# Down-projection weights of experts 0 to 14 loaded as full rows, their four column blocks combined together

## The reference, cut to what matters

```python
xe = jax.vmap(lambda hb, ib: hb[ib])(h, idx)                       # 16 experts x 32 tokens x 2048
hid = jax.nn.silu(jnp.einsum('becd,edf->becf', xe, w_gate)) * jnp.einsum('becd,edf->becf', xe, w_up)
ye = jnp.einsum('becf,efd->becd', hid, w_down) * gates[..., None]  # w_down: 16 x 1024 x 2048
# combine: zeros((n, d)).at[idx].add(ye); then h = h + mod[5] * that, and a last RMS norm
```

## Time and profile before

| | us |
|---|---|
| median of three runs | 1775.41 |
| lowest, highest | 1771.18, 1778.32 |
| span of the profiled execution (first to last instruction) | 1773.1 |
| PE busy | 1491.6 |
| DVE busy | 711.5 |
| ACT busy | 341.8 |
| POOL busy | 99.1 |

### The profile page before, as it was taken

How to read it: one execution, slowest core, us unless ns; L and a number is a source line. 1 busy time by engine, 2 the same in 40 slices (tenths; PEclk the granted TensorE clock), 3 DMA queues, 4 the chain that set the end, 5 groups by cost and what they waited for, 6 DMA issues and landing times.

```text
span 1773.1 us, 20259 instructions
## 1 busy us (share of the span) xinstructions
PE 1491.6 (84%) x7818; PEld 829.8 (47%) x7818; DVE 711.5 (40%) x1134; ACT 341.8 (19%) x591; POOL 99.1 (6%) x83
## 2 busy tenths in 40 slices
PE   2998999999999999998777788777887787877776
PEld 0557778877888777864122133211341232322112
DVE  1437677676767876653122032112211220321013
ACT  2433234233333345551000000000000000000001
POOL 0000000002340422000000000000000000000001
PEclk8999999999999999997887797778788877987787
DMA  9999656755746674578999999999999999999996
GB/s 340 381 363 267 240 193 240 277 195 201 250 166 235 208 269 149 191 308 312 420 416 416 417 419 416 415 418 419 415 416 419 418 416 415 419 417 416 417 420 253
DMA packets 155267, 593.24 MB, mean 335 GB/s; under 512 B 17838, under 2 KB 18214, under 8 KB 121390
## 3 DMA queue, kind: packets, MB, share of 16 engines
q1 hardware_dynamic: 144576, 580.95, 84.1%
q10 hardware_dynamic: 10606, 11.05, 2.1%
HBM read 589.80 MB, written 2.16 MB: 334 GB/s over the span
## 4 chain that ended last, share of the span: by engine, by line
PE 52%; DMA 33%; DVE 4%; SPq 4%; issue 2%; ACTq 2%; ACT 2%; POOL 0%; DVEq 0%; POOLq 0%
DMA ring_c<-in_w_up 10%; DMA ring<-in_w_up 10%; DMA ring_b<-in_w_down 8%; PE bank L530 7%; PE bank L532 7%; PE bank L531 7%; PE bank L849 5%; PE bank L784 4%; SPq L430 4%; PE bank L814 4%; DMA ring<-in_w_gate 2%; PE bank L526 2%; PE bank L835 2%; PE bank L528 2%; PE bank L527 2%; PE bank L775 2%
## 5 line engine op out<-in xcount | busy, mean ns | idle before, releaser
L814 PE MATMUL bank<-ring,xg 128*32 128x512 f32 x1536 | 243.7, 732 | 115.1 <-DMA ring<-in_w_gate 52.8
L1235 DVE TENSOR_TENSOR whl<-ring,whl 128x512 fp32r<-128x512 f32 x280 | 214.2, 769 | 150.8 <-ACT whl L916 150.0
L916 ACT ACTIVATE whl<-ring 128x512 fp32r<-128x512 f32 x280 | 176.3, 630 | 304.6 <-PE bank L532 237.2
L530 PE MATMUL bank<-whl,uh 128*128 128x512 f32 x512 | 209.8, 410 | 5.4 <-DVE vv L1262 1.7
L532 PE MATMUL bank<-whl,ul 128*128 128x512 f32 x512 | 200.3, 391 | 0.0
L531 PE MATMUL bank<-whl,uh 128*128 128x512 f32 x512 | 200.2, 391 | 0.0
L1531 DVE COPY gup<-bank 128x512 f32<-128x512 f32 x32 | 22.1, 691 | 440.8 <-PE bank L814 440.8
L814 PEld LDWEIGHTS bank<-ring,xg 128*32 128x32 f32 x1536 | 36.7, 117 | 289.3 <-DMA ring<-in_w_up 138.2
L1218 DVE SCALAR_TENSOR_TENSOR part<-ring,csT,part 128x1024 f32<-128x1024 f32 x120 | 160.4, 1336 | 0.1
L1125 ACT ACTIVATE gup<-bank 128x512 f32<-128x512 f32 x32 | 18.7, 597 | 635.4 <-PE bank L814 635.4
L784 PE MATMUL bank<-yy,gcur 128*128 128x512 f32 x256 | 122.6, 611 | 14.2 <-DVE yy L1542 14.2
(11 more groups left out here) (223 smaller groups left out, 1514.8 us busy)
## 6 DMA issues: line engine op xcount, KB each, us to landing
ring<-in_w_gate SPq DMA_DIRECT2D x128, 1024.0 KB, 20.6
ring<-in_w_mod SPq DMA_DIRECT2D x96, 1024.0 KB, 7.2
ring<-in_w_up SPq DMA_DIRECT2D x64, 1024.0 KB, 23.9
ring<-in_w_down SPq DMA_DIRECT2D x64, 1024.0 KB, 24.0
ring<-in_w_in SPq DMA_DIRECT2D x54, 1024.0 KB, 5.3
ring_b<-in_w_up SPq DMA_DIRECT2D x32, 1024.0 KB, 26.7
ring_c<-in_w_up SPq DMA_DIRECT2D x32, 1024.0 KB, 26.0
ring_b<-in_w_down SPq DMA_DIRECT2D x32, 1024.0 KB, 19.1
```

The source lines that it names most:

```text
L530: mm(ps, hi[:, k, cols], wh, start=k == 0, stop=False)
L814: last = mm(bank[2 * m + half][32 * quad:32 * quad + 32, :], xg[:, 2 * j + kk, CAP * ei:CAP * ei + CAP], w[:, kk, 512 * half:512 * half + ...
L916: a(whl[:, cidx % (AHEAD + 1), 0, :], slot_buf(slot[n])[:, 512 * (k % 4):512 * (k % 4) + 512], ACT.Copy).then_inc(hi_split, 1)
L1235: v.tensor_tensor(whl[:, cidx % (AHEAD + 1), 1, :], slot_buf(slot[n])[:, 512 * (k % 4):512 * (k % 4) + 512], whl[:, cidx % (AHEAD + 1), 0, ...
```

## The change

For experts 0 to 14 an item of `w_down` becomes 128 full rows: a partition takes one run of 8192 bytes, all four column blocks of one row of `w_down`. Its four matmuls write the four banks 0 to 3, a different group of rows in each, and the contraction over the 1024 rows is finished in all four banks only with item 23. So DVE weights all four blocks behind item 23, and all four combines follow there. The last expert keeps the old items, the old order and the old place of its combines. For this the group loop on PE and DVE runs three times, and the last group is written out behind it; the loop of SP is as before, and its last 8 issues use the old pattern.

```diff
-    wd_v = w_down[0].rearrange("e (r k p) (j n) -> e j r p k n", p=P, k=2, n=1024)
+    wd_v = w_down[0].rearrange("e (r p) n -> e r p n", p=P)
+    wd_last = w_down[0, E - 1].rearrange("(r k p) (j n) -> j r p k n", p=P, k=2, n=1024)
...
             if what == 2:
-                src = wd_v[bass.ds(e, 1), j // 4, j % 4]
+                sp.dma_start(slot_buf(s), wd_v[bass.ds(e, 1), j].rearrange("a p n -> (a p) n")).then_inc(ring_full[s], 16)
...
         for i in range(RING, 24):
             sp.wait_ge(moe_used, 24 * (E - 1) + i - RING + 1)
-            expert_item(E - 1, i)
+            if i < 16:
+                expert_item(E - 1, i)
+            else:
+                last_down_item(i - 16)
...
-        with pe.Fori(0, 4) as g:
+        def down_rows(g, ei):
+            for j in range(8):
+                s = moe_slots[(16 + j) % RING]
+                pe.wait_ge(ring_full[s], g * (16 * 8) + (fills[s] + 16 * (2 * ei + 2)))
+                for cb in range(4):
+                    quad = (j + cb) % 4
+                    last = mm(bank[cb][32 * quad:32 * quad + 32, :], hT[:, j, :], slot_buf(s)[:, 512 * cb:512 * cb + 512],
+                              start=j < 4, stop=j >= 4)
+                last.then_inc(moe_used, 1)
+            for cb in range(4):
+                combine(g, ei, cb)
...
+        with pe.Fori(0, 3) as g:
             pe.wait_ge(comb_add, g * 32 + 1)
             for ei in range(4):
...
+                expert(g, ei, down_rows)
+        pe.wait_ge(comb_add, 3 * 32 + 1)
+        for ei in range(4):
+            expert(3, ei, down_columns if ei == 3 else down_rows)
...
+        def down_rows(g, ei):
+            dve.wait_ge(moe_used, g * 96 + (24 * ei + 24))
+            for cb in range(4):
+                weighted(cb)
+            for cb in range(4):
+                scattered(g, ei, cb)
```

More of the change, by code:

```diff
@@ new lines, in down_columns @@
+        def down_columns(g, ei):
+            for j in range(8):
+                half, r = j // 4, j % 4
+                s = moe_slots[(16 + j) % RING]
+                pe.wait_ge(ring_full[s], g * (16 * 8) + (fills[s] + 16 * (2 * ei + 2)))
+                w = slot_buf(s).rearrange("p (k c) -> p k c", k=2)
+                for n in range(2):
+                    for kk in range(2):
+                        quad = 2 * ((r + n) % 2) + kk
+                        last = mm(bank[2 * half + n][32 * quad:32 * quad + 32, :], hT[:, 2 * r + kk, :],
+                                  w[:, kk, 512 * n:512 * n + 512], start=r < 2, stop=r >= 2)
+                last.then_inc(moe_used, 1)
+                if j in (5, 6):
+                    combine(g, ei, j - 5)
+            combine(g, ei, 2)
+            combine(g, ei, 3)
@@ L854, in _ @@
-                combine(g, ei, 2)
-                combine(g, ei, 3)
+                expert(g, ei, down_rows)
+        pe.wait_ge(comb_add, 3 * 32 + 1)
+        for ei in range(4):
+            expert(3, ei, down_columns if ei == 3 else down_rows)
     @block.scalar
@@ new lines, in expert @@
+        def expert(g, ei, down):
+            for m in range(2):
+                dve.wait_ge(moe_used, g * 96 + (24 * ei + 8 * m + 8))
+                if m == 0:
+                    dve.wait_ge(summed, g * 4 + (ei + 1))
+                v.tensor_copy(gup[:, 2 * m + 1, :], bank[2 * m + 1][:, :]).then_inc(gu_dve, 1)
+            dve.wait_ge(g_pe, g * 4 + (ei + 1))
+            dve.wait_ge(comb, g * 32 + (8 * ei + 1))
+            v.tensor_copy(gcur[:, :], bank[5][:, 0:SEQ]).then_inc(g_ok, 1)
+            dve.wait_ge(silu_ok, g * 4 + (ei + 1))
+            v.tensor_tensor(hT[:, :, :], sgate[:, :, :], bank[4][:, SEQ:512].rearrange("p (f n) -> p f n", f=FC),
+                            ALU.mult).then_inc(hid_ok, 1)
+            down(g, ei)
@@ L1550, in _ @@
+        with dve.Fori(0, 3) as g:
+            tokens_of(g)
+            for ei in range(4):
+                expert(g, ei, down_rows)
+        tokens_of(3)
+        for ei in range(4):
+            expert(3, ei, down_columns if ei == 3 else down_rows)
         dve.wait_ge(comb_add, E * 8 + 1)
```

85 lines of the change are left out of this document (62 added, 23 removed).

## The result

| | before | after |
|---|---|---|
| median, us | 1775.03 (8 runs, 1771.18 to 1783.38) | 1763.91 (8 runs, 1761.20 to 1772.22) |
| span of the profiled execution, us | 1773.1 | 1763.4 |

The ratio is 0.9947, with a 95% interval from 0.9931 to 0.9963: 9.4 us faster, between 6.6 and 12.2. The forecast was 1767 us. The profiled execution took 1765.14 us as a whole, 1.7 us more than its span.

A forecast was written before the change was run, and what follows sets the result against it. From about 840 us the DMA loads of expert weights set the time. The down loads save 8.5 us and all else counts 0: 1775.4 - 8.5 = 1766.9, rounded 1767 us; own range 1763 to 1771, 8 in 10 within 1762 to 1773.

The forecast's parts named there:

- The term of the loads: Down loads of experts 0 to 14: 420.7 instead of 409.0 GB/s saves 0.57 us an expert, 8.5 us in all.
- Rival 1: Down loads: 4096-byte packets are slower for another reason than size, so no gain, 1775.4 us; chance 0.09.
- Rival 2: End of the loads: engines finish more evenly, 8.5 + 4.9 us gained, 1762.0 us; chance 0.09.
- The two rules of the Trainium skill: Down loads: line rate from 512 bytes means no gain; fixed overhead a packet means 1.5%, 4.7 us.
- Late combines: From last down matmuls to next gate matmul: 9.1 us instead of 5.37, made good within the gate part, cost 0.
- Cover at a group's start: Starts of groups 1 to 3: 11.5 us of queued work, 3.7 go, 7.8 stay, cost 0.
- SP's issue of a down load: SP's queue: issue falls from a median of 4.16 us to about 1 us, gain 0.
- The uneven end: Last expert's loads, where the engines do not finish together: counted 0, with 3 us put into the range.
- The median: Timed runs: the saving carries over to the median, 1775.4 - 8.5 = 1766.9, rounded 1767 us.

The follow-up runs named there:

- run 1: Changed kernel with its new order of work, but down items of experts 0 to 14 fetched as two runs of 4096 bytes a partition: 1774.32 us, ratio 0.9994.
- run 2: Kernel before with its old order of work, but down items of experts 0 to 14 fetched as full rows of 8192 bytes: 1764.86 us, ratio 0.9940.
- run 3: Changed kernel's order of work, with gate, up and down items all fetched as two runs of 4096 bytes: 1800.14 us, ratio 1.0132.
- run 6: Changed kernel with the first combine matmul of experts 0 to 14 issued eight times more: 1765.24 us, ratio 0.9951.
- run 7: Changed kernel with the first combine matmul of experts 0 to 14 issued sixteen times more: 1794.10 us, ratio 1.0106.
- run 5: Changed kernel with the last expert also taking full rows and late combines: 1768.01 us, ratio 0.9966.
- run 4: Changed kernel with all items but the last expert's down fetched in pairs, 16384 bytes a partition, tokens in steps of 4: 1777.25 us, ratio 1.0012.
- run 8: Changed kernel with only the down items of experts 0 to 14 fetched in pairs, 16384 bytes a partition: 1761.25 us, ratio 0.9935.

## Why the prediction was right, step by step

- **The term of the loads**, 8.5 us (7.3 to 9.5): 8.8 and 8.8 us in the stage of two profiled executions of after, against one of before; 9.4 and 10.8 us by the two ratios. Runs 1 and 2 show that it is the pattern of the loads alone. Rival 1 (another cause behind the 409) falls with run 1, where the moved work stayed and the rate fell back, and with the last expert, whose old pattern still reads 407 to 410.
- **Rival 2**, an end that finishes more evenly, 13.4 us in all: it lies outside the first ratio's 6.6 to 12.2 us, and the falling end is no shorter. The median of 1763.91 is nearer to its 1762 than to 1767, but by the spread of medians, not by its mechanism.
- **The two rules of the Trainium skill.** By the 512-byte rule of the Trainium skill's "DMA: Bandwidth & Descriptors", Specifications, runs 1, 2 and 3 should all have taken the time of before; they lie between -0.6% and +1.3%. The fixed overhead that the same page of the Trainium skill gives in "Why small descriptors are slow (HBM only)" has the right sign, and half of the size: 409 against 421 GB/s is 2.9%, not 1.5%.
- **Late combines**, forecast 9.1 us between the parts, measured 8.7 at seven experts and 10.3 to 10.7 at five. The row above is one of the five: 8.74 us for the eight combines where twice 3.69 was worked out. The granted clock is 0.60 in their first 3.5 us (1205.0 to 1208.5) and 0.95 behind. Before them PE had waited for three loads (0.47, 1.41 and 1.42 us). At the seven the clock is 1.0. That PE has caught up with the loads and idles before the last items is what the step had not priced; it makes this way 1.6 to 2.0 us longer and costs no time.
- **Cover at a group's start**, forecast 11.5 - 3.7 = 7.8 us left, measured 14.22 - 4.7 = 9.5 in this execution and 10.7 - 4.7 = 6.0 in after's second one (a load issued at 1052.7 us), so the forecast lies between them. The chains show that the delay was partly paid out of PE's waits: before, PE reached the down part's end behind its loads, now it waits for the last down load until 1265.2. Cost 0 holds, and runs 6 and 7 bracket it: 7 us more are borne, 14 are not.
- **SP's issue of a down load**, forecast near 1 us from 4.16, measured 1.9. The cost (0) is right, the reading is not. The 4.16 us are the median of the loads into `ring` alone; those into `ring_b` and `ring_c` took 2.20 and 2.16 before and take 2.00 and 2.01 now, with half of the packets. In run 3, where every load has 256 packets, the three are 2.13, 2.36 and 2.23. So an issue is not held in proportion to its own packets. All these medians but the 4.16 lie between 1.9 and 2.4 us, and the engines need 2.5 us for 1 MiB at 421 GB/s. That would fit a full queue that takes a load in as one moves out, but no run isolates it. The 0.88 us of the gate loads in the earlier trace rows, the prediction's measure, are 0.33 us now.
- **The uneven end**, 0 with 3 us either way: the fall from 407 to 19 GB/s takes about as long as before, and run 5 shows that the old place of the last combines saves 3.4 to 5 us there.
- **The median.** 1763.91 is 3 us below 1767. By the ratio, 1775.4 x 0.9947 = 1766.0, so most of this is the spread of medians: the first matmul of the stage starts between 803 and 810 us in executions whose first 800 us are the same code (in run 3 at 811, without its wait). The 3 us of allowance were of the right size. That the ratio's 9.4 us came within 1 us of 8.5 says little by itself, with an interval of 6.6 to 12.2; the stage's 8.8, seen twice, says more.

What stays open is why a larger packet moves faster. The runs give 409, 421 and 427 GB/s for 4096, 8192 and 16384 bytes, and they can't tell a fixed time per packet from one per run of addresses in memory, since both changed together. A fixed 0.009 us for each, worked out from the first two rates before run 4, gave the third as 427. The 16384-byte loads also come as DMAs of 2 MiB instead of 1 MiB, which no run holds fixed; between 4096 and 8192 bytes the DMAs are 1 MiB each.

## What to carry to other kernels

Where the DMA engines are full all through a stage, lay the weights out so that a partition's run is as long as can be, even if compute has to move for it: in this kernel 8192 instead of 4096 bytes is worth 2.9% of the rate, 16384 another 1.4%. Check what the new layout does to the other operands: in run 4 a step of 16 bytes ate the gain. Before moving work behind the last load of a round, read the cover: the time from issue to landing of the tightest load, less the landing on an empty queue. Work below it was free here; the cover itself differed by 3.5 us between two executions of one kernel, so leave that much. At the very end of a kernel there is no cover, so the last round keeps its early combines.

## What the runs showed of the hardware

- A single core, the whole stage long: 409 GB/s with 4096-byte packets (run 3), 421 with 8192 (run 2, after), 427 to 429 with 16384 in DMAs of 2 MiB (run 4, in the slices where the queue stays full).
- Loading a 128 x 128 fp32 stationary operand at the full granted clock: 196 ns with a step of 8 bytes, 329 ns with 16. At half the clock 331 and 330 ns.
- An issue on a full queue holds SP for about 2 us (medians of 1.9 to 2.4, for 128 and for 256 packets; 4.2 for the loads into `ring` in the kernel before). With pairs (128 packets of 16384 bytes, half as many issues) it is 0.33 us, here in run 8:

```profile
L431 SPq DMA_DIRECT2D ring<-in_w_down x30: 327/333/896, 817.4 to 1640.4; - x30
```
